# A hybrid recurrence and attention block: attention values as weights, probabilities scaled before they are mixed, low-rank products between two banks

## The reference, cut to what matters

```python
logits = einsum('bcqhgd,bckhd->bhgcqk', qc, kb) * (HEAD_DIM ** -0.5)   # 8 query heads, 2 key heads, 64 wide
logits = where(valid, logits + bias, NEG_INF)                         # own chunk of 64 and the one before
probs = softmax(concatenate([logits, sink], -1), -1)[..., :KEY_BAND]
out = einsum('bhgcqk,bckhd->bcqhgd', probs, vb)
y = concatenate([y_rwkv, y_att], -1) @ w_out
```

## Time and profile before

| | |
|---|---|
| time, median of 3 runs | 2751.17 us (2746.04 to 2753.61) |
| profiled execution | 2746.87 us, its span 2745.0 us |
| PE busy | 2440.1 us, 89% of the span |
| DVE busy | 1125.5 us, 41% |
| ACT busy | 757.2 us, 28% |
| POOL busy | 391.6 us, 14% |
| mean granted TensorE clock | 0.945 |

### The profile page before, as it was taken

The page is one execution under the profiler, slowest core; times in us unless marked ns, Lnnn a source line. Parts: engine busy times, 40 slices in busy tenths (PEclk is TensorE's granted clock), DMA queues, the critical chain, the costliest instruction groups (busy, mean ns, idle before and its releaser), DMA issues. The chain is left out here.

```text
span 2745.0 us, 67296 instructions
## 1 busy us (share of the span) xinstructions
PE 2440.1 (89%) x27710; PEld 1532.4 (56%) x27711; DVE 1125.5 (41%) x2596; ACT 757.2 (28%) x1815; POOL 391.6 (14%) x481
## 2 busy tenths in 40 slices
PE   3999999999997799999999997389999999998970
PEld 1878788788785667777777674223333333232320
DVE  0355656556556345656565654411111111111118
ACT  0244353443443112222223231012222212121212
POOL 0111111111111211212121220001011101010100
PEclk8999999999998899999999997589999999999985
DMA  8012121121123552131222221565535386999959
GB/s 329 9 59 81 47 87 53 47 93 47 52 81 140 225 191 105 72 118 72 102 80 99 90 87 39 232 281 222 229 138 229 137 347 232 396 361 405 375 227 368
DMA packets 54675, 451.78 MB, mean 165 GB/s; under 512 B 7932, under 2 KB 8992, under 8 KB 32576
## 3 DMA queue, kind: packets, MB, share of 16 engines
q1 hardware_dynamic: 36504, 390.71, 36.2%
q0 software_dynamic: 10656, 38.80, 3.7%
q10 hardware_dynamic: 7304, 19.19, 1.9%
HBM read 367.41 MB, written 87.56 MB: 166 GB/s over the span
## 5 line engine op out<-in xcount | busy, mean ns | idle before, releaser
L1741 PE MATMUL ps<-arena 128*32 128x512 f32 x4608 | 514.5, 604 | 24.7 <-DMA arena<-wex 15.2
L1741 PEld LDWEIGHTS ps<-arena 128*32 128x32 f32 x4608 | 150.4, 111 | 382.0 <-issue 367.5
L452 PE MATMUL ps<-arena 128*128 128x128 f32 x3072 | 354.1, 276 | 2.2 <-ACT arena L594 2.1
L452 PEld LDWEIGHTS ps<-arena 128*128 128x128 f32 x3072 | 348.5, 192 | 13.3 <-ACT arena L594 13.3
L1096 PE MATMUL ps<-arena 64*64 64x64 f32 x8704 | 297.2, 221 | 31.5 <-issue 9.6
L1096 PEld LDWEIGHTS ps<-arena 64*64 64x64 f32 x8704 | 277.0, 136 | 60.8 <-issue 59.7
L1755 PE MATMUL ps<-arena 128*32 128x512 f32 x2304 | 267.3, 605 | 7.4 <-DMA arena<-wex 5.8
L1241 PE MATMUL ps<-arena 128*128 128x512 f32 x512 | 239.1, 611 | 0.7 <-ACT arena L1318 0.7
L1961 DVE TENSOR_TENSOR arena<-arena,ps 128x256 f32<-128x256 f32 x72 | 29.9, 416 | 461.7 <-ACT arena L1799 461.7
L463 PE MATMUL ps<-arena 128*128 128x512 f32 (+1 forms) x512 | 213.5, 555 | 0.0
L1799 ACT ACT_TABLE_LOAD x36 | 46.2, 1283 | 584.6 <-PE ps L1741 584.6
(11 more groups left out here) (327 smaller groups left out, 2991.8 us busy)
## 6 DMA issues: line engine op xcount, KB each, us to landing
arena<-wex SPq DMA_DIRECT2D x105, 2048.0 KB
mid<-arena SPq DMA_DIRECT2D x16, 2568.0 KB, 8.5
arena<-mid SPq DMA_DIRECT2D x16, 2568.0 KB, 9.6
arena<-ada SPq DMA_DIRECT2D x12, 2048.0 KB, 9.5
arena<-y SPq DMA_DIRECT2D x16, 1024.0 KB, 7.2
arena<-x SPq DMA_DIRECT2D x31, 512.0 KB, 5.6
arena<-w_in SPq DMA_DIRECT2D x8, 1232.0 KB, 24.6
arena<-x ACTq DMA_DIRECT2D x17, 512.0 KB, 10.4
```

The source lines that it names most:

```text
L452: mm = pe.matmul(bank[name][0:m, at:at + P], V["w_in"][:, kk, w0:w0 + m], V["hT"][:, kk, :], start=(kk == 0), stop=(kk == KD - 1))
L1741: mm = pe.matmul(bank[("HA", "HB")[g]][rows[j], :], xT[:, kk, rows[j]], slot[j][:, at:at + 2 * FH], start=(kk == 0), stop=(kk == KD - 1))
```

## The change

Six edits are made together.

1. In `att5` the roles are swapped: the values (128x64) are the weights and two heads' transposed probabilities (256 columns) move. The heads of T0 write PSUM partitions 0 to 63, those of T1 partitions 64 to 127, in turn. `ya` is then already transposed, four products a group in place of eight.
2. The scaling by the softmax sum moves ahead of the transposes: a new step `pn_0`, `pn_1` on VectorE adds, takes the reciprocal and multiplies the probabilities of a group in place (128x4x192), and `att4` waits for it (`pn`) in place of `probs`.
3. In the order, `pn_0` stands behind `exp_0` and so ahead of `ev_v`, `pn_1` behind `att4_0`. At the end VectorE only copies C2.
4. In `lora1`, products of `w2` and `a2` alternate between C0 and C1, and both banks are marked full behind the last.
5. In pass 2, `yT` transposes only the recurrence's half; ScalarE copies `ya` from SBUF, and a semaphore `yaT` tells TensorE and the loader.
6. The rows of `w_out` are put in the order of the new `ya` on the host.

```diff
-("tok1", 0), ("exp_0", 0), ("in_kv2", 1), ("ev_v", 1), ("tok2", 0), ("ev_l", 1), ("att3_1", 0), ("att4_0", 0), ("exp_1", 0),
+("tok1", 0), ("exp_0", 0), ("pn_0", 0), ("in_kv2", 1), ("ev_v", 1), ("tok2", 0), ("ev_l", 1), ("att3_1", 0), ("att4_0", 0), ("pn_1", 0), ("exp_1", 0),
...
 def lora1(t, b):
+    B.wait_free(pe, "C1", "za", t)
     for c in range(CC):
-        mm = pe.matmul(bank["C0"][...], w2[0:32], tw[0:32])
-    B.full(mm, "C0")
-    B.wait_free(pe, "C1", "za", t)
-    for c in range(CC):
-        mm = pe.matmul(bank["C1"][...], w2[32:64], f[32:64])
-    B.full(mm, "C1")
+        zw = pe.matmul(bank["C0"][...], w2[0:32], tw[0:32])
+        za = pe.matmul(bank["C1"][...], w2[32:64], f[32:64])
+    B.full(zw, "C0")
+    B.full(za, "C1")
...
 def att4(g):
-        S.wait(pe, "probs", 2 * t + g + 1)
+        S.wait(pe, "pn", 2 * t + g + 1)
 def att5(g):
-        for i in range(4):
-            h = 4 * g + i
-            B.wait_read(pe, f"T{i // 2}", f"P{g}", t)
-            for part in range(2):
-                mm = pe.matmul(bank["C2"][:, 64 * h:64 * h + 64], V["PT"][:, i, P * part:P * part + P], v,
+        for half in range(2):
+            B.wait_read(pe, f"T{half}", f"P{g}", t)
+        for part in range(2):
+            for half in range(2):
+                mm = pe.matmul(split(bank["C2"][64 * half:64 * half + 64, 256 * g:256 * g + 256], 2), v,
+                               V["PT"][:, 2 * half:2 * half + 2, P * part:P * part + P],
...
+def probs(g):                                   # VectorE, steps pn_0 and pn_1
+        S.wait(dve, "probs", 2 * t + g + 1)
+        dve.tensor_tensor(V["den"][:, g4], V["sm"][:, g4], V["es"][:, g4], ALU.add)
+        dve.drain()
+        dve.reciprocal(V["den"][:, g4], V["den"][:, g4])
+        dve.drain()
+        keys = V["Pm_v"][:, :, 64:256]
+        dve.tensor_tensor(keys, keys, per_channel(V["den"][:, g4], KEYS), ALU.mult).then_inc(S["pn"], 1)
 def att5(t, b):                                 # VectorE
-        (add, reciprocal)
         S.wait(dve, "pv", 2 * t + 2)
-        dve.tensor_tensor(split(pk["ya"], QH), split(bank["C2"][:, :], QH), per_channel(V["den"], HD), ALU.mult)
+        dve.tensor_copy(pk["ya"], bank["C2"][:, :])
...
 def yT(t, b):                                   # pass 2, ScalarE
+        act.activation(W["yT"][:, 4:KD, :], split(W["pk"][b]["ya"], 4), ACT.Copy).then_inc(S["yaT"], 1)
         act.activation(W["yT"][:, 0:4, :], split(bank["O0"][:, :], 4), ACT.Copy)
```

More of the change, by code:

```diff
@@ L477, in lora1 @@
                 B.wait_free(pe, "C0", "zw", t)
-                for c in range(CC):
-                    mm = pe.matmul(bank["C0"][:, P * c:P * c + P], V["w2"][0:32, P * c:P * c + P], V["tw"][0:32, :],
-                                   start=True, stop=True)
-                B.full(mm, "C0")
                 B.wait_free(pe, "C1", "za", t)
                 for c in range(CC):
-                    mm = pe.matmul(bank["C1"][:, P * c:P * c + P], V["w2"][32:64, P * c:P * c + P],
+                    zw = pe.matmul(bank["C0"][:, P * c:P * c + P], V["w2"][0:32, P * c:P * c + P], V["tw"][0:32, :],
+                                   start=True, stop=True)
+                    za = pe.matmul(bank["C1"][:, P * c:P * c + P], V["w2"][32:64, P * c:P * c + P],
                                    V["f"][b][32:64, 3 * CC, :], start=True, stop=True)
-                B.full(mm, "C1")
+                B.full(zw, "C0")
+                B.full(za, "C1")
                 B.wait_free(pe, "C2", "gate", t)
@@ L559, in go @@
                     B.wait_read(pe, "C2", "gate", t)
-                    for i in range(4):
-                        h = 4 * g + i
-                        B.wait_read(pe, f"T{i // 2}", f"P{g}", t)
-                        for part in range(2):
-                            v = V["qkv"][b if part else 1 - b][:, 640 + 64 * g:704 + 64 * g]
-                            mm = pe.matmul(bank["C2"][:, 64 * h:64 * h + 64], V["PT"][:, i, P * part:P * part + P], v,
+                    for half in range(2):
+                        B.wait_read(pe, f"T{half}", f"P{g}", t)
+                    for part in range(2):
+                        v = V["qkv"][b if part else 1 - b][:, 640 + 64 * g:704 + 64 * g]
+                        for half in range(2):
+                            mm = pe.matmul(split(bank["C2"][64 * half:64 * half + 64, 256 * g:256 * g + 256], 2), v,
+                                           V["PT"][:, 2 * half:2 * half + 2, P * part:P * part + P],
                                            start=(part == 0), stop=(part == 1))
@@ L851, in att4, with go @@
                 return go
-            def att5(t, b):
[L854 to L858, removed]
+            def probs(g):
+                def go(t, b):
+                    S.wait(dve, "probs", 2 * t + g + 1)
+                    g4 = slice(4 * g, 4 * g + 4)
+                    dve.tensor_tensor(V["den"][:, g4], V["sm"][:, g4], V["es"][:, g4], ALU.add)
[4 more added lines that the diff above has]
+                    dve.tensor_tensor(keys, keys, per_channel(V["den"][:, g4], KEYS), ALU.mult).then_inc(S["pn"], 1)
+                return go
+            def att5(t, b):
                 S.wait(dve, "pv", 2 * t + 2)
-                dve.tensor_tensor(split(pk["ya"], QH), split(bank["C2"][:, :], QH), per_channel(V["den"], HD), ALU.mult).then_inc(S["ya"], 1)
+                dve.tensor_copy(pk["ya"], bank["C2"][:, :]).then_inc(S["ya"], 1)
             run(dve, {"norm": norm, "ev_r": ev("r"), "ev_k": ev("k"), "ev_v": ev("v"), "ev_lora": ev("lora"),
                       "att1": att1, "kk": kk, "ew2": ew2, "ew3": ew3, "tok1": tok("tokB"), "tok2": tok("tokV"),
-                      "att3_0": att3(0), "att3_1": att3(1), "att4_0": att4(0), "att4_1": att4(1), "att5_1": att5})
+                      "att3_0": att3(0), "att3_1": att3(1), "pn_0": probs(0), "pn_1": probs(1), "att4_0": att4(0),
+                      "att4_1": att4(1), "att5_1": att5})
 def views(nc, ctx):
@@ L1028, in load @@
                 B.wait_full(sp, "O0", "yT", n - 2)
+                S.wait(sp, "yaT", n - 1)
                 if n >= 2:
@@ L1224, in yT @@
                     pe.wait_ge(S["mod_added"], MOD1 + MODS)
[L1225 to L1231, removed]
+                B.wait_free(pe, "O0", "yT", t)
+                S.wait(pe, "yr", t + 1)
+                for c in range(CC):
+                    mm = pe.transpose(bank["O0"][:, P * c:P * c + P], W["yc"][:, P * c:P * c + P], ident)
+                B.full(mm, "O0")
             def o(n0, kk):
@@ L1238, in go @@
                             pe.wait_ge(S["w_out"], 32)
-                        for other in ("O0", "O1"):
-                            B.wait_read(pe, other, "yT", t)
+                        B.wait_read(pe, "O0", "yT", t)
+                        S.wait(pe, "yaT", t + 1)
+                        B.wait_free(pe, name, "o", t)
                     mm = pe.matmul(bank[name][:, :], W["yT"][:, kk, :], W["w_out"][:, kk, 512 * n0:512 * n0 + 512],
@@ L1315, in yT @@
             def yT(t, b):
-                for i, name in ((1, "O1"), (0, "O0")):
-                    B.wait_full(act, name, "yT", t)
-                    B.free(act.activation(W["yT"][:, 4 * i:4 * i + 4, :], split(bank[name][:, :], 4), ACT.Copy), name)
+                S.wait(act, f"pack{b}", 16 * (t // 2) + 16)
+                B.wait_full(act, "O1", "o", t - 1)
+                act.activation(W["yT"][:, 4:KD, :], split(W["pk"][b]["ya"], 4), ACT.Copy).then_inc(S["yaT"], 1)
+                B.wait_full(act, "O0", "yT", t)
+                B.free(act.activation(W["yT"][:, 0:4, :], split(bank["O0"][:, :], 4), ACT.Copy), "O0")
             def norm2(t, b):
@@ L2060, in in_columns, with out_rows @@
     return np.concatenate([w[:, :3 * C], w[:, RW_COLS:], w[:, 3 * C:RW_COLS]], 1)
+def out_rows(w):
+    att = w[C:].reshape(KVH, 2, 2, HD, D).transpose(0, 2, 1, 3, 4).reshape(QH * HD, D)
+    return np.concatenate([w[:C], att], 0)
 def host_arrays(inputs):
```

6 lines of the change are left out of this document (3 added, 3 removed).

## The result

The changed kernel takes 2775.62 us (median of 4 runs, 2770.1 to 2776.34), the kernel before 2751.28 us (median of 4). The ratio is 1.0096 with a 95% interval of 1.0082 to 1.0109: slower by 24 us, where a gain of 4 was forecast.

The account below looks back on a forecast made before the run. TensorE, busy 592.85 of 600 us in pass 1, was taken as the bound; -5.7 (pass 1), +2.0 (last tile) and -0.5 (pass 2) gave -4.2 us, 2742.7 against the profiled execution, 2747 as median, range 2741 to 2752.

Parts of the forecast that it names:

- the late T1: In pass 1, T1 comes free 0.85 us late, so the second half of att4_0 moves by the full 0.85.
- the last tile: Last tile of pass 1: nothing covers VectorE's added scaling; with a faster last group, together +2.0 us.
- the rivals: Cheap collision, 0.10; TensorE bounds pass 2, 0.10; column tiles not side by side, 0.04; late ev_v costs more, 0.16.
- The sum of a tile without a fall: Each of 15 tiles in pass 1: -1.28 + 0.85 + 0.05 = -0.38 us.
- the collision: VectorE's group 0 multiplication and GpSimd's subtraction L717 exclude each other: ev_v 1.0 or 0.70 us late, 0.85 taken.
- the rest: Per tile of pass 1 without the collision: 1.28 us won, less 0.05 for waiting on VectorE's copy of T1.
- The products of the values: In att5, two column tiles side by side: 1.00 us a group plus 0.09 to enter, for 1.73; 0.64 won.
- Rival (c): Column tiles in att5 don't run side by side: a tile costs 1.34 us more, total +22, 2773 us; chance 0.04.
- The low-rank products: In lora1, alternation is worth nothing under ScalarE's last eviction; without that cover 0.7 us a tile.
- Pass 2: Four fewer transposes only fill a wait that stays; the scan starts 0.26 us behind the copy; -0.5 us in all.
- 0.13 for slower: Chance of over 0.3% slower: rival (c), part of the dearer late ev_v, and a corner of the forecast.

Follow-up runs that it names:

- e1: Kernel before with only the scaling steps pn_0 and pn_1 put ahead of the transposes, all else old: 2768.11 us, ratio 1.0062.
- e6: Changed kernel with two of the eight products of the next tile's q projection moved ahead of att4_0 on TensorE: 2753.4 us, ratio 1.0019.
- e11: Changed kernel with four transposes of the attention, which nothing reads, put back into pass 2 on TensorE: 2768.12 us, ratio 1.0077.
- e2: Changed kernel without the multiplication that scales the probabilities: pass 1 725.4 us in one execution, usual period 48.78 us.
- e3: Changed kernel with the low-rank products as before, four into C0, then four into C1: 2772.6 us, ratio 1.0069.
- e7: e4 with the four evictions of T1 behind the next tile's transposes moved from ScalarE to VectorE: 2720.18 us, ratio 0.9903.
- e8: e7 with the low-rank products as before the change: 2729.12 us, ratio 0.9934.
- e4: Changed kernel with the step ev_v moved ahead of exp_0 in the order: 2728.49 us, ratio 0.9926.

## Why the prediction was wrong, point by point

- **The step that failed** is the price of the late T1: "the second half of `att4_0`, which already waits for exactly that the earlier trace rows, moves by the full 0.85". The move was right, but I took its length as its whole price and kept the full granted clock of the earlier trace rows for what stands behind it. The runs showed that the longer wait can bring the clock down, and each fall costs another 1.6 us: 1.21 in the projection (4.81 less 3.60) and 0.45 in the transposes (1.11 less 0.66). There were 14 falls. With 14 times 1.6, -0.38 in 15 tiles and the +2.0 of the last tile the sum is 19, and 19.3 was measured (15.8 and 3.5; the fourteenth fall lies in the second part). None of the rivals named it. That e1 (scaling alone) shows the fall and e6 (work in the wait) doesn't shows that the wait brings it about. The length of the wait doesn't fix the number of falls, though: e11, with the same pass 1, had nine in its 15 tiles, and e1 four.
- **The sum of a tile without a fall** was right: -0.38 forecast, 49.56 against 49.95 measured in e11, -0.39. Its terms: the collision costs 0.78 (e1), forecast 0.85; the rest gains 1.17 (e2), forecast 1.23.
- **The products of the values**: 1.01 us from start to next start, forecast 1.00; 0.10 to enter, forecast 0.09. Together 0.62 won a group, forecast 0.64. Rival (c) would have given nearly the measured time, 2773, but for a wrong reason: the two column tiles do run side by side.
- **The collision**: right. VectorE came first, by 0.03 us. GpSimd ended 0.89 behind the multiplication's end instead of 1.13, so the delay was 0.78 instead of 1.0.
- **The low-rank products**: nothing under ScalarE's cover (e3), right. Without the cover 0.55 (e7, e8), forecast 0.7.
- **Pass 2**: right. The same 0.25 us, and 0.4 once.
- **The last tile**: the stretch from the last start on L439 to the scan grew by 3.5 us, where the forecast has +2.0 and the -0.38 of the fifteenth tile, together +1.6. The fall behind the fifteenth tile's wait (856.47 us) lies in it and is 1.6 of the difference; the 1.9 left is near the forecast. Most of the last tile runs at half speed in both kernels: the mean granted clock is 0.60 from 865 to 909 us, and 0.71 in the like stretch before (848 to 890). Its end:

```profile
903.00:910.00 7.00, 4.36 (x30) 2.88 (x32) 1.47 (x3) 0.60 (x1) 0.11 (x1) 0.50 0.16 68
```

- **The chances**: 0.13 for slower rested on mechanisms that cost what they are long. That a longer wait could also cost granted clock, which the earlier trace rows had at 1.00 throughout, had no chance of its own.

## What to carry to other kernels

Where TensorE is busy nearly always, read a new wait on it twice: once for its length, and once for what the granted clock does behind it. Look at the windows right behind the longest wait. Two products moved into the wait took the fall away in e6, 1.8 us a tile in pass 1, but not the collision; moving `ev_v` ahead (e4) took the wait itself away, 2.9 us a tile. And before an operation of VectorE with two operands in SBUF is placed into a gap of its own, see whether GpSimd works in that gap: an order that moved GpSimd's part earlier turned a loss of 24 us into a gain of 21.

## What the runs showed of the hardware that I had not expected

- A wait of 1.34 us on TensorE, in a tile in which it is busy about 48 of 50 us, was followed in some tiles by a granted clock of 0.50, and by 1.00 in others, with the same instructions around it (the two tiles of e1). A wait of 0.56 in the kernel before and one of 0.92 in e6 were followed by no fall in any of the 15 tiles.
- Once it has begun, it can come back in every tile (the changed kernel, e3, e11): 1.6 us each, a period of 51.2 in place of 49.56 us, to the end of pass 1. In e1, whose tiles are 50.73 us long, it came back only after 204.84, 153.74 and 153.69 us, near multiples of the same 51.2.
- A VectorE operation on four elements of each partition, with one input, took 0.96 us in place of 0.17 while GpSimd worked on two operands in SBUF (L840 in e4). The Trainium skill, "SBUF — State Buffer", section "Who interferes with whom", counts `tensor_scalar` among the operations that can take the shared port pair; this row agrees.
